# Feed-forward of a one-core streaming encoder layer in float32: the 128x128 turns of the hidden activations change from TensorE to VectorE and device memory

## The reference

```python
def squared_relu_mlp(h, w1, w2):
    return jnp.square(jax.nn.relu(h @ w1)) @ w2

...
        x = x + squared_relu_mlp(rms_norm(x, norm_ffn_g[l]), w_ff1[l], w_ff2[l])
    return rms_norm(x, final_norm_g)
```

## Time and profile before

| | us |
|---|---|
| median of 3 runs | 1646.04 (1643.89 to 1647.24) |
| the profiled execution, its own time | 1646.18 |
| its span (first to last instruction) | 1644.4 |
| TensorE busy in it | 1627.2 (99%) |
| VectorE, ScalarE, GpSimd busy | 1088.3, 811.9, 98.0 |
| DMA queue of SyncE, share of the 16 DMA engines | 59.2% |

### The profile page before, as it was taken

How to read it: one execution, slowest core, us unless ns; L and a number is a source line. 1 busy time by engine, 2 the same in 40 slices (tenths; PEclk the granted TensorE clock), 3 DMA queues, 4 the chain that set the end, 5 groups by cost and what they waited for, 6 DMA issues and landing times.

```text
span 1644.4 us, 21894 instructions
## 1 busy us (share of the span) xinstructions
PE 1627.2 (99%) x7524; PEld 1358.0 (83%) x7524; DVE 1088.3 (66%) x1476; ACT 811.9 (49%) x1063; POOL 98.0 (6%) x187
## 2 busy tenths in 40 slices
PE   9999999999999999999998999999999999999998
PEld 7888888888888888888887888888888888888886
DVE  5688988888888898665555655555555455545554
ACT  6444456555555556743445644434443444334443
POOL 6500011211111000000000000000000000000000
PEclk9999999999999999999999999999999999999999
DMA  7666655555555666557563566566656665566554
GB/s 249 207 185 187 190 160 159 174 169 181 172 155 172 221 201 182 189 180 268 177 194 115 168 182 190 191 194 190 186 188 191 191 182 188 193 192 184 192 184 142
DMA packets 158953, 304.91 MB, mean 185 GB/s; under 512 B 11658, under 2 KB 15874, under 8 KB 158466
## 3 DMA queue, kind: packets, MB, share of 16 engines
q1 hardware_dynamic: 157504, 299.41, 59.2%
q0 software_dynamic: 1056, 3.46, 0.6%
q10 hardware_dynamic: 320, 1.06, 0.2%
HBM read 301.78 MB, written 2.10 MB: 185 GB/s over the span
## 4 chain that ended last, share of the span: by engine, by line
PE 97%; ACT 1%; DVE 1%; issue 0%; POOL 0%; POOLq 0%; ACTq 0%
PE ps L1267 30%; PE ps L1269 30%; PE ps L1268 30%; PE ps L1280 2%; PE ps L1451 1%; PE ps L1450 1%; ACT hconv L750 0%; PE ps L1467 0%; PE ps L1461 0%; PE ps L1304 0%; PE ps L1555 0%; PE ps L1584 0%; PE ps L1583 0%; PE ps L1582 0%; PE ps L1468 0%
## 5 line engine op out<-in xcount | busy, mean ns | idle before, releaser
L868 DVE TENSOR_TENSOR wlo<-raw,whi 128x1024 fp32r<-128x1024 f32 x560 | 685.7, 1228 | 410.1 <-ACT whi L535 404.7
L535 ACT ACTIVATE whi<-raw 128x1024 fp32r<-128x1024 f32 x560 | 591.1, 1060 | 569.7 <-PE ps L1269 561.8
L1267 PE MATMUL ps<-whi,a_hi 128*128 128x512 f32 x1244 | 490.7, 394 | 0.6 <-issue 0.6
L1269 PE MATMUL ps<-whi,a_lo 128*128 128x512 f32 x1244 | 484.7, 390 | 0.0
L1268 PE MATMUL ps<-wlo,a_hi 128*128 128x512 f32 x1244 | 484.3, 389 | 0.0
L1267 PE MATMUL ps<-whi,c_hi 128*128 128x512 f32 x752 | 293.8, 391 | 0.0
L1269 PE MATMUL ps<-whi,c_lo 128*128 128x512 f32 x752 | 292.7, 389 | 0.0
L1268 PE MATMUL ps<-wlo,c_hi 128*128 128x512 f32 x752 | 292.6, 389 | 0.0
L1269 PEld LDWEIGHTS ps<-whi,a_lo 128*128 128x128 f32 x1244 | 233.5, 188 | 49.1
L1267 PEld LDWEIGHTS ps<-whi,a_hi 128*128 128x128 f32 x1244 | 233.7, 188 | 47.8 <-DVE wlo L868 1.2
L1268 PEld LDWEIGHTS ps<-wlo,a_hi 128*128 128x128 f32 x1244 | 233.8, 188 | 46.7
(11 more groups left out here) (240 smaller groups left out, 1081.8 us busy)
## 6 DMA issues: line engine op xcount, KB each, us to landing
raw<-in_w_ff_dram SPq DMA_DIRECT2D x256, 512.0 KB, 4.1
raw<-in_w_in_dram SPq DMA_DIRECT2D x144, 512.0 KB, 3.7
raw<-in_w_mla_out_dram SPq DMA_DIRECT2D x32, 512.0 KB, 4.6
raw<-in_w_conv_out_dram SPq DMA_DIRECT2D x32, 512.0 KB, 4.1
raw<-in_w_out_dram SPq DMA_DIRECT2D x32, 512.0 KB, 4.6
raw<-in_w_ukv_dram SPq DMA_DIRECT2D x16, 512.0 KB, 3.6
raw<-in_w_xkv_dram SPq DMA_DIRECT2D x16, 512.0 KB, 4.2
raw<-in_w_uq_dram SPq DMA_DIRECT2D x16, 384.0 KB, 3.7
```

The source lines that it names most:

```text
L535: act.activation(whi[:, s, :], raw[:, s, :], ACT.Copy).then_inc(hi_ready, 1)
L868: dve.tensor_tensor(wlo[:, s, :], raw[:, s, :], whi[:, s, :].bitcast(F32), ALU.subtract).then_inc(lo_ready, 1)
L1267: pe.matmul(sum_, x_hi[:, k0 + k, tok], w_hi, start=(first and k == 0), stop=False)
L1269: mm = pe.matmul(sum_, x_lo[:, k0 + k, tok], w_hi, start=False, stop=(last and k == kts - 1))
```

## The change

TensorE's turns in the feed-forward go. In their place:

1. right after the square, VectorE transposes all 32x32 blocks of the 256x512 chunk by two block-transpose instructions (one per 128 tokens) into `blocks`; each block is then right in itself, but lies on the wrong partitions;
2. SyncE stores `blocks` (512 KB) to `bounce`, a scratch tensor in device memory;
3. when that has landed, SyncE reads it back by four loads of 128 KB, each for 32 partitions of `moved`;
4. ScalarE copies `moved` to `c_hi` and VectorE writes `c_lo` (two instructions of 128x512 each, as before, but from SBUF and after k = 4 in place of k = 3);
5. TensorE's waits in chunk 4 are for a whole chunk of `c_lo` at even k.

In SyncE's program the store for chunk c stands behind the first weight load of chunk c + 2, and the four loads behind the second, where SyncE waits for the store to land. The diff, cut to its core:

```diff
+        blocks = at(o, "blocks", [P, QUADS, CPB, TT, QUAD])
+        moved = at(o + 4096, "moved", [P, QUADS, CPB, TT, QUAD])
+        bounce = nc.dram_tensor("bounce", [P, QUADS, CPB * TT * QUAD], F32, kind="Internal").ap()
...
+        def quads(dst, c, t):
+            return dst[:, 4 * c:4 * c + 4, P * t:P * (t + 1)].rearrange("p k (i e) -> p k i e", i=QUADS)
...
+            def store_blocks(g, c):
+                sp.wait_ge(blocks_ready, g * CH + (c + 1))
+                sp.dma_start(bounce[:], blocks[:].rearrange("p j k t e -> p j (k t e)")).then_inc(blocks_stored, 16)
+            def move_blocks(g, c):
+                sp.wait_ge(blocks_stored, g * (16 * CH) + 16 * (c + 1))
+                for j in range(QUADS):
+                    sp.dma_start(moved[QUAD * j:QUAD * (j + 1), :, :, :, :].rearrange("p i k t e -> p i (k t e)"),
+                                 bounce[:, j, :].rearrange("(i p) n -> p i n", i=QUADS)).then_inc(blocks_moved, 16)
...
-                    load_chunk(U_FF + UPC * c, r, w_ff1, g * D + NC * c)
+                    for k in range(UPC):
+                        load(U_FF + UPC * c + k, r, w_ff1[:, 2 * k:2 * k + 2, ds(g * D + NC * c, NC)])
+                        if k == 0 and c >= 2:
+                            store_blocks(g, c - 2)
+                        if k == 1 and c >= 2:
+                            move_blocks(g, c - 2)
...
                         load(U_FF + UPC * (CH + c) + k, r, w_ff2[:, ds(g * KT + 2 * k, 2), NC * c:NC * (c + 1)])
+                        if k == 0 and c < 2:
+                            store_blocks(g, c + 2)
+                        if k == 1 and c < 2:
+                            move_blocks(g, c + 2)
...
-                        if k == 3 and c:
-                            turn_out(g * CH + (T_FF + c - 1), c_hi, 4 * (c - 1))
+                        if k == 4 and c:
+                            moved_out(g, c - 1)
...
+            def moved_out(g, c):
+                act.wait_ge(blocks_moved, g * (16 * QUADS * CH) + 16 * QUADS * (c + 1))
+                for t in range(TT):
+                    act.activation(quads(c_hi, c, t), moved[:, :, :, t, :].rearrange("p i k e -> p k i e"), ACT.Copy).then_inc(turn_hi, 1)
...
+            def moved_low(g, c):
+                for t in range(TT):
+                    dve.wait_ge(turn_hi, g * (2 * CH) + (2 * (T_FF + c) + t + 1))
+                    dve.tensor_tensor(quads(c_lo, c, t), moved[:, :, :, t, :].rearrange("p i k e -> p k i e"),
+                                      quads(c_hi, c, t).bitcast(F32), ALU.subtract).then_inc(turn_lo, 1)
...
                     dve.tensor_tensor(rows[:, p, :, :], rows[:, p, :, :], rows[:, p, :, :], ALU.mult).then_inc(chunk_out, 1)
+                    dve.wait_ge(chunk_out, g * (2 * CH) + (N_FF + c + 1))
+                    dve.wait_ge(blocks_moved, g * (16 * QUADS * CH) + 16 * QUADS * c)
+                    for t in range(TT):
+                        turned_blocks = dve.transpose(blocks[:, :, :, t, :].rearrange("p j k e -> p k j e"),
+                                             rows[:, p, t, :].rearrange("p (k j e) -> p k j e", k=CPB, j=QUADS))
+                    turned_blocks.then_inc(blocks_ready, 1)
...
-                        if c == CH:
-                            pe.wait_ge(turn_lo, g * (2 * CH) + (2 * splits_before(T_FF) + k + 1))
+                        if c == CH and k % 2 == 0:
+                            pe.wait_ge(turn_lo, g * (2 * CH) + (2 * splits_before(T_FF) + k + 2))
...
-                        if k == 3 and 1 <= c <= CH:
-                            pe.wait_ge(chunk_out, g * (2 * CH) + n)
-                            turn(None, rows[:, pair_of(n - 1), :, :], 0,
-                                 (turn_lo, g * (2 * CH) + (2 * splits_before(T_FF + c - 2) + 1)))
```

More of the change, by code:

```diff
@@ L36 @@
 XH = 4
+QUAD = 32
+QUADS = P // QUAD
 DFF = 4 * D
@@ L329, in build @@
         tail_rooted, tail_rs, tail_gained = (sem(n) for n in ("tail_rooted", "tail_rs", "tail_gained"))
+        blocks_ready, blocks_stored, blocks_moved = (sem(n) for n in ("blocks_ready", "blocks_stored", "blocks_moved"))
         fin_act, fin_dve, stored = sem("fin_act"), sem("fin_dve"), sem("stored")
+        def quads(dst, c, t):
+            return dst[:, 4 * c:4 * c + 4, P * t:P * (t + 1)].rearrange("p k (i e) -> p k i e", i=QUADS)
         block = ctx.enter_context(nc.Block())
@@ L831, in ff_group @@
                             hi(U_FF + UPC * (CH + c) + k + LEAD, r)
-                        if k == 3 and c == 0:
-                            turn_out(g * CH + (T_FF + CH - 1), c_hi, 4 * (CH - 1))
+                        if k == 4 and c == 0:
+                            moved_out(g, CH - 1)
                     if last and c < CH - 1:
@@ L1215, in ff_group @@
                             reciprocal(rs_2, sd_n, R_2)
-                        if k == 3 and c:
-                            turn_low(g * CH + (T_FF + c - 1), c_lo, c_hi, 4 * (c - 1))
+                        if k == 4 and c:
+                            moved_low(g, c - 1)
                     p = pair_of(N_FF + c)
@@ L1224, in ff_group @@
                             lo(U_FF + UPC * (CH + c) + k + LEAD, r)
-                        if k == 3 and c == 0:
-                            turn_low(g * CH + (T_FF + CH - 1), c_lo, c_hi, 4 * (CH - 1))
+                        if k == 4 and c == 0:
+                            moved_low(g, CH - 1)
                         if last and k == 4 and c:
```

## The result

The changed kernel takes **1657.61 us** (median of 4 runs, 1656.09 to 1659.37) against 1645.62 us for the kernel before on the same chip (4 runs, 1643.89 to 1647.24): a ratio of **1.0077, 95% interval 1.0065 to 1.0089**, 12 us slower. I had forecast 1640 and a range that ended at 1652. The profiled execution took 1656.09 us.

The account below looks back on a forecast made before the run. TensorE, busy 1627.2 of 1644.4 us, was taken to bound the kernel. From 1646.18 us, 14.1 saved on turns and 7.6 added by waits gave 1639.6, rounded to 1640; the range was 1634 to 1652.

Parts of the forecast that it names:

- What goes: In the feed-forward, 16 turns of 0.88 us each leave TensorE: 14.1 us, all on the path.
- Block transposes: On VectorE after the square, two of 128x512 at 0.65 us each; ends 0.48 and 1.23.
- The place in the queue: On SyncE, the store is issued 6.95 us after chunk 4's first matmul, behind the first load of chunk 5.
- The store: 512 KB to device memory lands at 11.6 us, behind a load landing at 10.3; ends 10.6 and 12.4.
- Four loads: Read-back issued from 11.75 us on, 0.40 apart; the last takes 3.3 us to land, ends 2.6 and 3.8.
- The Trainium skill's rule on the ports of 32 partitions: For the read-back, 512 KB would take 2.6 us, not 1.3; the sum would be 2.2 us worse.
- M and the wait: Read-back landed at M = 16.25 us; TensorE idle 1.9 us before unit 6 of chunk 4, 7.6 in four groups.
- What is hidden: Chunks 0 to 2, turned during chunks 1 to 3, cost nothing if the read-back lands by 18.2 us.
- Rival 3: Round trip ends after 18.2 us, so chunks 1 to 3 also delay TensorE; slower, 1655 us; chance 21%.
- The clock: After idle time before unit 6 of chunk 4, TensorE's clock may halve: 1.7 us each, 6.8 for four.
- rival 2: Gain given back through slower transposes, TensorE's clock or slower read-back loads; 1644.3 or 1646 us; chance 29%.

Follow-up runs that it names:

- hybrid: Changed kernel, but chunk 3 of each group turned by TensorE inside chunk 4 as before; 1634.84 us, ratio 0.9934.
- the fifth experiment, experiment 5: Changed kernel with the store ahead of the chunk's last weight load, the four loads right behind that load; 1630.03 us, ratio 0.9911.
- experiment 9: Changed kernel with the store right behind the chunk's last weight load, the four loads behind the next chunk's first load; 1637.90 us, ratio 0.9961.
- experiments 1 to 3: Kernel before plus the new chain, unread: 1644.49 us; hybrid: 1634.84 us; changed kernel plus 20 useless matmuls before unit 6 of chunk 4: 1651.47 us.
- experiment 6: Changed kernel with only the store moved, ahead of the chunk's last weight load, the four loads left in place; 1654.37 us, ratio 1.0059.
- experiment 8: Changed kernel with the store issued from ScalarE's own DMA queue after its weight copy of unit 5; 1650.55 us, ratio 1.003.
- experiment 4: Changed kernel with the store ahead of the chunk's last weight load, the four loads behind the next chunk's first load; 1638.65 us, ratio 0.9963.

## Why the prediction was wrong

- **What goes: right.** 14.1 us; hybrid gave 10.8 of 10.6, and the fifth experiment 14.3 of 14.1.
- **Block transposes: right.** 0.65 us predicted, 0.69 measured:

```profile
L1265 DVE STREAM_TRANSPOSE blocks<-rows x32: 668/692/714, 948.0 to 1557.1; 128x512 f32<-128x512 f32 x32
```

- **The place in the queue: right in time, wrong in company.** The store was issued at 7.0 to 7.1 us (once at 7.2, once at 7.5), 6.95 predicted. But I counted one weight load ahead of it. The splits of units 3 and 4 follow each other at once after the transposes, so two weight loads are released 1.13 us apart (1196.91 and 1198.04), the second just ahead of the store. I had both splits in the sum and drew from them only when the store could go, not what went with it.
- **The store: this step failed.** 4.65 us with an upper end of 12.4 - 6.95 = 5.45. Measured 5.2 to 6.9 in chunks 0 to 2 (mean 6.0) and 7.1 to 8.6 for chunk 3 (mean 7.6), which alone decides. My 4.65 was made of two terms: the load ahead lands 3.75 us after its issue, and the store 1.3 us behind it. The second was right, 1.25 to 1.31 us sixteen times. The first failed: that load took 4.4 to 6.1 us in chunks 0 to 2 and 6.3 to 7.8 in chunk 3 (mean 6.8). A third of this could have been read beforehand: in the kernel before, the same load of chunk 5 took 4.7 to 4.9 us in the four groups, and it already stood 1.4 us behind another. Here it is in the second group, first before, then in the changed kernel:

```profile
L345 SPq DMA_DIRECT2D raw<-in_w_ff_dram x1: 372/372/372, 1198.1 to 1198.1; - x1
...
DMA to landing us min/median/max: 4.7/4.7/4.7
```

```profile
L354 SPq DMA_DIRECT2D raw<-in_w_ff_dram x1: 373/373/373, 1198.0 to 1198.0; - x1
...
DMA to landing us min/median/max: 7.8/7.8/7.8
```

  The other 2 us come with the change: the weight load before it is 1.1 us ahead and not 1.4, and the store follows 0.5 us behind. The store alone slows a load ahead of it by some 0.7 us: in experiment 9 that load took 4.2 to 4.7 us, where the same load before took 3.6 to 4.0. By experiments the 2.9 us in all split roughly so: one load ahead costs 5.3 and not 4.65 (+0.65), the second about 0.9 more, `w_ff2`'s loads 1.25 more. My bounds came from transfers that stood alone or between loads that nothing waited for the earlier trace rows; none of these rows was a store in traffic, I took 3.75 us for a load whose median in the earlier trace rows is 4.2, and 0.8 us was too little for an unseen thing.
- **Four loads: a little better than predicted.** 3.3 us for the last; measured 2.4 to 3.4, median 2.8. The Trainium skill's rule on the ports of 32 partitions (SBUF — State Buffer, "Door 1: The DMA port swizzle") would have made this step longer, and it was shorter. Whether the loads moved at a lower rate is not settled by that: they are issued 0.38 to 0.47 us apart and in the second group land 0.59, 0.46 and 0.61 us apart, where my estimate by that rule has 0.65 a load.
- **M and the wait: the formula held.** Idle time = M + 1.95 - 16.32. M was 18.78, 19.95, 19.11 and 18.27 us in the four groups, which gives 4.41, 5.58, 4.74 and 3.90; measured 4.33, 5.57, 4.73 and 3.82. With M at 16.25 I had 7.6 us in all, and it was 18.45.
- **What is hidden: right.** Chunks 1 to 3 show no idle time, with M up to 18.1, one of them practically at the limit of 18.2 that I had worked out; no run went beyond it there. Rival 3 expected these chunks to pay as well, and they did not. It had named the tipping point, a wait of 3.5 us, and all four waits are above it.
- **The clock: left out of the sum.** I had it as a way into rival 2, 1.7 us a time, and against it that TensorE is dense before unit 6. The sum put it at nothing. Measured: 1.6 to 2.3 us more than usual behind each wait, 7.1 in all. The size from the earlier trace rows was right; that density beforehand protects was wrong. It is also not independent of the wait, as I had treated it: a longer wait brings the slower clock with it.

So the sum with the measured terms: -14.1 + 18.45 + 7.1 = +11.4. Of the 17.6 us between 1640.0 and 1657.6, about 10.9 are the longer wait and 7.1 the clock. The wait was the one I forecast; the size of one term, and the clock that the sum left out, turned the sign.

The Trainium skill (VectorE: DVE Perf Modes, "Rules for kernel authors") advises turning 128x128 on TensorE where the result may lie in PSUM. In this kernel TensorE is the bound, and moving the turns off it won 14.3 us once the chain ended in time (experiment 5).

## What to carry to other kernels

The time of a transfer that is waited for depends on what was issued just ahead of it: look up which transfers the same event releases there, and place it ahead of them, both the store and the loads that read it back. Price it by the landing of the transfer ahead of it, read from the trace at that very place and not from the median of all. Here the same instructions cost +0.77% or gained 0.89%, by their place among the weight loads alone. And if TensorE is the bound and must wait, add what its clock takes afterwards: a wait of 4.6 us on average cost TensorE 6.4.

## What the runs showed of the hardware that I had not expected

- A 512 KB store took 2.7 us with no weight load just ahead, less than the 3.6 us of the earlier trace rows, but 5.3 us behind one load of its own queue (median), 5.5 behind one of another queue, and 6.2 behind two.
- Behind two loads it landed 1.23 to 1.31 us after the load just ahead of it, in all 60 stores of the change and experiments 1 to 3, whether that load took 4.0 us or 7.8.
- Four loads of 128 KB, 2.8 us each in the change, took up to 8.5 us behind weight loads (experiment 6): in these runs the small transfers were held up as much as the large ones.
- The half clock follows an idle time even where TensorE was dense before it. After 2.19 us (experiment 8) the granted clock fell,

```profile
1388.72 0.49 PE L1321 MATMUL ps<-whi,c_hi 128*128 128x512 f32 x1 [2.19 <-DVE c_lo L1242]
```

```profile
1388.80:1390.80 2.00, 2.00 (x6) 1.63 (x7) 2.00 (x2) 0.88 (x1) 0.00 (x0) 0.62 0.00 0
```

and after 2.26 us (experiment 4) it did not:

```profile
1204.46 0.49 PE L1314 MATMUL ps<-whi,c_hi 128*128 128x512 f32 x1 [2.26 <-DVE c_lo L1235]
```

```profile
1204.00:1209.00 5.00, 4.54 (x20) 3.77 (x21) 3.09 (x4) 2.49 (x3) 0.00 (x0) 1.00 0.36 121
```

In the feed-forward's traces it fell after every idle time of 2.36 us and more, and after none of 1.88 us and less. What decides between is open.

**Open** are also why the load ahead slows down where a store follows it, why `w_ff2`'s loads are slower, and what exactly the store and the loads share behind the queues. A store from GpSimd's queue was not tried.
